# Two-block transformer kernel: norms transposed by a product with a diagonal, scale and shift applied by channel in the split

## The chip, the cores and the metric

The kernel runs as one program on one core of a Trainium2 chip. The metric is the device time of the program in microseconds (us), lower is better. The engines are named as in the profile: PE is TensorE (matmuls), DVE is VectorE, ACT is ScalarE, POOL is GpSimd, SP is SyncE, which here only issues the large weight loads.

## The reference, cut to what matters

Two blocks work on 256 tokens of 1024 channels in float32, one after the other. What is computed, cut to the norms and what stands between them:

```
# block 1, two layers
for l in range(2):
    y = token_mixer(x, ...)                        # attention and mLSTM
    x = layer_norm(ALPHA*x + y, ln_g[l,0], ln_b[l,0])
    y = swiglu(x, w13, w2) if l == 0 else moe_ffn(x, router_w, router_b, exp_w13, exp_w2)
    x = layer_norm(ALPHA*x + y, ln_g[l,1], ln_b[l,1])
# block 2, two layers
for l in range(2):
    x = x + mixer2(rms_norm(x, norm_mix_g[l]))     # conv, attention, gated linear attention
    x = x + conv_ffn(rms_norm(x, norm_ffn_g[l]))
return rms_norm(x, final_g)

layer_norm: (x - mean) * rsqrt(var + eps) * g + b      rms_norm: x * rsqrt(mean(x*x) + eps) * g
```

The mean and variance are taken over the 1024 channels of a token; `g` and `b` are vectors by channel. `moe_ffn` sends each token to 2 of 8 experts by `x @ router_w`.

## The kernel before

**Tiling.** `x` lies in SBUF as two tiles (`t` = 0, 1) of 128 tokens by 1024 channels. A quarter is one `t` and one half `h` of 512 channels (`QUARTERS`). Weights come from HBM in units of 128 partitions by 2048 floats into a ring of six (`raw`, issued by SP, L401), and every unit is split in two f32r parts: `w_hi` by an ACT copy (L1315) and `w_lo` by a DVE subtraction (L1702), in rings of three. `x` is transposed and split likewise into `xT_hi` and `xT_lo`, eight chunks of 128 channels. Every product is three f32r matmuls, hi by hi, lo by hi, hi by lo (L619 to L621).

**Order.** Each engine's instructions stand in the order in which the code writes them; there is no scheduler. Engines meet by semaphores: PE may not start a transpose before `xn_ready`, ACT copies what PE has put in PSUM (`xT_psum`), DVE subtracts what ACT has copied (`xT_hi_ready`), PE takes a chunk when `xT_lo_ready` says so. Splits of the next weight units (`split`) stand between this work at places chosen by hand: `split_next` on ACT splits three units ahead before a norm, and `ahead(14)` splits one before a norm of block 2.

**The norm sites.** Eight places have a norm. After each of them but the last `transpose_x` (L653) has PE make 16 transposes of 128x128 pieces against the identity (`ident`, part of the constants in `cst`) into four PSUM banks, and `x_parts` on ACT (L1330) and DVE (L1712) splits them, four instructions of 128x512 on each. The text calls the sites by letters:

| site | place | norm | about us |
|---|---|---|---|
| A | layer 0 of block 1, after the mixer, ahead of the dense FFN | LayerNorm | 218 |
| B | layer 0 of block 1, after the dense FFN, ahead of the next mixer | LayerNorm | 419 |
| C | layer 1 of block 1, after the mixer, ahead of the router | LayerNorm | 621 |
| D | end of the experts, and entry of block 2 | LayerNorm, then rms norm | 1680 |
| E | layer 0 of block 2, ahead of the conv FFN | rms norm | 1835 |
| F | entry of layer 1 of block 2 | rms norm | 2038 |
| G | layer 1 of block 2, ahead of the conv FFN | rms norm | 2183 |
| H | end of the program | rms norm | 2385 |

**LayerNorm** (`layer_norm`, L1741): after the statistics DVE makes (x - mean) * g on the two quarters of half 0 (`centred`, L1752), takes the reciprocal of the root that ACT made (L1763), makes x * rstd + b on half 0 (`finished`, L1757), and then both for half 1. Each half releases eight transposes. **rms norm** (`rms_norm`, L1770): after each addition of a PSUM quarter to x (L1796) DVE squares and sums that quarter (`mean_square`, L1738); then it adds up the sums (L1773), waits for ACT's root (L1340) and writes `xn` = x * rstd * g, four instructions of 128x512 (L1782), which PE transposes.

**The router** at site C: PE multiplies `xT` by the router's weights, ACT copies the logits (L1504), DVE works out the two experts of every token (L2022 on), and PE gathers the tokens of each expert by a product of `x` with a 0/1 matrix `pick` (L994). This gather is a plain float32 matmul. Ahead of L2022, DVE's queue holds `x_parts` and one weight split.

**Small loads** are issued by POOL in the order of L535 to L606: rows of weights by name into `rows`, `w_if` (runs of four floats), gains and shifts of the norms into `norm_gb` broadcast to all partitions, and the constants of block 2. Most wait for `xn_ready`.

## Time and profile before

| | us |
|---|---|
| the three runs | 2386.18, 2396.31, 2385.08 |
| median | 2386.18 |
| the profiled execution: its own time | 2396.32 |
| its span, first to last instruction | 2394.5 |
| PE busy in it | 2283.5 (95%) |
| DVE busy | 1746.6 (73%) |
| ACT busy | 1322.0 (55%) |
| POOL busy | 181.6 (8%) |
| DMA packets | 423432 for 556.44 MB, 9746 of them under 512 B |

Busy time is the union of an engine's instructions; a busy PE need not be at full speed, since the clock that it was granted is shown beside it (1.00 is 2.4 GHz, 0.50 is 1.2 GHz). A row of the timeline begins with the start in us and the length of the row in us, and ends with the idle time ahead of it and what ended that. A plain float32 matmul leaves two records on PE, so that `x32` at L994 stands for 16 matmuls; a transpose, and each f32r matmul, leaves one.

### The profile page before, as it was taken

What the parts mean: (1) busy time and instruction counts of PE and PEld (TensorE: products, weight loads), DVE (VectorE), ACT (ScalarE), POOL (GpSimd) and SP (SyncE); (2) the same over time, 40 slices, a digit from 0 to 9 for tenths busy, and PEclk for the clock granted to TensorE, in tenths of its full rate; (3) what the DMA queues carried; (4) which work ended last, traced back from release to release, by engine and by line L of the source; (5) the groups of instructions that cost most, each with busy time, mean ns of one, the idle gap of its engine ahead of it and who ended that gap; (6) DMA issues with size and microseconds to landing.
All of it is one profiled execution on the core that took longest, in us unless ns stands there. A gap on an engine that the chain in (4) does not pass through costs nothing.

```text
span 2394.5 us, 41114 instructions
## 1 busy us (share of the span) xinstructions
PE 2283.5 (95%) x16253; PEld 2135.1 (89%) x16253; DVE 1746.6 (73%) x1872; ACT 1322.0 (55%) x1254; POOL 181.6 (8%) x178
## 2 busy tenths in 40 slices
PE   7998999999799999999999999999699999898998
PEld 7998998899799999999999999998687999787997
DVE  4565555557588888888888888887667777767777
ACT  4643433454366767676767776766425444425443
POOL 1000000100000000000000000000580000760000
PEclk9998999999899999999999999999879999989999
DMA  9344655534399999999999999999323555423541
GB/s 304 108 142 141 206 181 175 172 108 143 124 356 335 355 338 349 337 351 336 353 343 348 345 341 349 336 353 329 112 92 117 174 195 174 132 93 126 197 173 56
DMA packets 423432, 556.44 MB, mean 232 GB/s; under 512 B 9746, under 2 KB 377092, under 8 KB 423344
## 3 DMA queue, kind: packets, MB, share of 16 engines
q1 hardware_dynamic: 419232, 544.85, 67.4%
q0 software_dynamic: 4112, 10.38, 1.4%
q8 instruction: 60, 0.98, 0.2%
q14 instruction: 28, 0.23, 0.0%
HBM read 554.13 MB, written 1.06 MB: 232 GB/s over the span
## 4 chain that ended last, share of the span: by engine, by line
issue 45%; PE 42%; DVE 7%; ACT 3%; DVEq 2%; DMA 1%; ACTq 0%; SPq 0%; POOL 0%; POOLq 0%
PE ps L619 12%; PE ps L620 12%; PE ps L621 12%; DVE w_lo L1702 2%; ACT w_hi L1315 2%; PE ps L1191 1%; PE ps L661 1%; DVE cvT L2174 0%; PE ps L1189 0%; DVEq L2175 0%; PE ps L810 0%; DMA raw<-in_w_in 0%; DVE xn L1738 0%; DVE x L1796 0%; PE ps L802 0%
## 5 line engine op out<-in xcount | busy, mean ns | idle before, releaser
L1702 DVE TENSOR_TENSOR w_lo<-raw,w_hi 128x2048 fp32r<-128x2048 f32 x519 | 1180.6, 2285 | 347.1 <-ACT w_hi L1315 345.5
L1315 ACT ACTIVATE w_hi<-raw 128x2048 fp32r<-128x2048 f32 x519 | 987.0, 1908 | 250.7 <-PE ps L621 236.4
L619 PE MATMUL ps<-w_hi,xg_hi 128*128 128x256 f32 x1792 | 516.7, 288 | 2.2 <-DVE w_lo L1702 2.2
L621 PE MATMUL ps<-w_hi,xg_lo 128*128 128x256 f32 x1792 | 505.0, 282 | 0.0
L620 PE MATMUL ps<-w_lo,xg_hi 128*128 128x256 f32 x1792 | 504.8, 282 | 0.0
L619 PE MATMUL ps<-xT_hi,w_hi 128*128 128x256 f32 (+1 forms) x1712 | 493.5, 288 | 11.5 <-DVE xT_lo L1712 6.7
L620 PE MATMUL ps<-xT_lo,w_hi 128*128 128x256 f32 (+1 forms) x1712 | 488.5, 285 | 0.0
L621 PE MATMUL ps<-xT_hi,w_lo 128*128 128x256 f32 (+1 forms) x1712 | 488.2, 285 | 0.0
L619 PEld LDWEIGHTS ps<-xT_hi,w_hi 128*128 128x128 f32 (+1 forms) x1712 | 331.8, 194 | 16.6 <-issue 8.6
L619 PEld LDWEIGHTS ps<-w_hi,xg_hi 128*128 128x128 f32 x1792 | 338.1, 189 | 9.4 <-DVE xg_lo L2086 2.9
L620 PEld LDWEIGHTS ps<-w_lo,xg_hi 128*128 128x128 f32 x1792 | 338.3, 189 | 3.8
L621 PEld LDWEIGHTS ps<-w_hi,xg_lo 128*128 128x128 f32 x1792 | 338.0, 189 | 0.0
L620 PEld LDWEIGHTS ps<-xT_lo,w_hi 128*128 128x128 f32 (+1 forms) x1712 | 331.6, 194 | 1.6
L621 PEld LDWEIGHTS ps<-xT_hi,w_lo 128*128 128x128 f32 (+1 forms) x1712 | 331.2, 193 | 0.3
L619 PE MATMUL ps<-w_hi,hT_hi 128*128 128x512 f32 x536 | 212.8, 397 | 1.0 <-DVE hT_lo L2095 1.0
L620 PE MATMUL ps<-w_lo,hT_hi 128*128 128x512 f32 x536 | 212.0, 396 | 0.0
L621 PE MATMUL ps<-w_hi,hT_lo 128*128 128x512 f32 x536 | 211.6, 395 | 0.0
L619 PE MATMUL ps<-w_hi,xT_hi 128*128 128x256 f32 (+1 forms) x448 | 130.4, 291 | 7.9 <-DVE w_lo L1702 4.3
L620 PE MATMUL ps<-w_lo,xT_hi 128*128 128x256 f32 (+1 forms) x448 | 128.3, 286 | 0.0
L621 PE MATMUL ps<-w_hi,xT_lo 128*128 128x256 f32 (+1 forms) x448 | 128.2, 286 | 0.0
L621 PEld LDWEIGHTS ps<-w_hi,hT_lo 128*128 128x128 f32 x536 | 100.9, 188 | 23.8
L1517 ACT ACTIVATE sa<-ps 128x256 f32<-128x256 f32 x112 | 43.1, 385 | 139.3 <-PE ps L621 139.2
(441 smaller groups left out, 2774.2 us busy)
## 6 DMA issues: line engine op xcount, KB each, us to landing
raw<-in_exp_w SPq DMA_DIRECT2D x336, 1024.0 KB, 6.0
raw<-in_ffn_w_up SPq DMA_DIRECT2D x44, 1024.0 KB, 5.1
raw<-in_w_in SPq DMA_DIRECT2D x42, 1024.0 KB, 6.7
raw<-in_ffn_w SPq DMA_DIRECT2D x33, 1024.0 KB, 5.1
raw<-in_ffn_w_down SPq DMA_DIRECT2D x22, 1024.0 KB, 5.4
raw<-in_w_gate SPq DMA_DIRECT2D x16, 1024.0 KB, 5.3
raw<-in_w_out SPq DMA_DIRECT2D x8, 1024.0 KB, 5.1
raw<-in_w_o SPq DMA_DIRECT2D x6, 1024.0 KB, 6.1
```

The costliest lines, as they stand in the source:

```text
L619: pe.matmul(out, lhs[0], rhs[0], start=first, stop=False)
L620: pe.matmul(out, lhs[0], rhs[1], start=False, stop=False)
L621: return pe.matmul(out, lhs[1], rhs[0], start=False, stop=last)
L661: m = pe.transpose(o[:, c, t, :], src[:, t, (2 * b + c) * P:(2 * b + c + 1) * P], ident)
L1191: m = pe.matmul(o, qgm[rows, h // 2, t, j, :], st8[rows, 4 * t + j, h // 2, :], start=False, stop=j == 3)
L1315: act.activation(w_hi[:, u.const % SPL, 0:width], raw[:, u.const % RAW, 0:width], ACT.Copy)\
L1517: act.activation(sa[:, odd, 0:FFC], ps[:, 6, 0:FFC], ACT.Silu).then_inc(S_.silue_ready, 1)
L1702: dve.tensor_tensor(w_lo[:, u.const % SPL, 0:width], raw[:, u.const % RAW, 0:width], w_hi[:, u.const % SPL, 0:width].bitcast(F32), ALU.sub ...
```

## The change

What it does, by place:

- **PE**: `transpose_x` takes `x` itself, and in place of a transpose against the identity it makes a plain float32 matmul of the piece with `dg[:, t, :]`, a 128x128 diagonal that holds the token's rstd. The very first one of the program (block 1, layer 0) keeps the transpose.
- **DVE, LayerNorm**: (x - mean) * g is made as before. After the first half come two diagonals (`diagonals`), not `finished(0)`. `finished` of all four quarters (`normed_x`) stands behind `x_parts`: right behind it at A and C, behind one more `split` at B.
- **DVE, rms norm**: squares and the four `xn` products go (at H the four products stay); DVE takes one reciprocal and makes one diagonal for each `t`.
- **ACT**: `square_roots` loads the table by a root of a constant, then squares and sums each quarter (Square with an accumulated sum) when DVE has added it, and takes the root.
- **x_parts**: on both engines eight instructions of 128x256, not four of 128x512 (on DVE at the program's start it stays four), with the shift `beta` or the gain `gain` of the channel as bias or scale.
- **D**: the last LayerNorm of block 1 (`last_layer_norm`) releases ACT's squares after each quarter, in the order (0,0), (1,0), (0,1), (1,1).
- **Splits on ACT**: one fewer stands ahead of the norm at B, E, F and G, and that split comes behind `x_parts`.
- **POOL**: four loads of gains to `norm_gb` go, each with its wait; seven loads of vectors by channel (128x8, one float a run) come at the program's start, into `stat`. The loads of the next norm's gain and shift wait for `ln_done`, the load of `final_g` for nothing.
- `zeros`, the width of `stat`, the counts of roots, and some `sem_inc`s whose counts nothing reads are changed as follows from this.

```diff
+            dg = sb("dg", [P, TT, P], scope=shared)
 ...
+                if L == 0:
+                    column = lambda dst, v: pool.dma_start(dst, v.rearrange("(c p) -> p c", p=P), allow_slow_non_contiguous=True)                        .then_inc(S_.beta_loaded, 16)
+                    for n, v in enumerate((A["ln_b"][0, 0], A["ln_b"][0, 1], A["ln_b"][1, 0])):
+                        column(beta(n), v)
+                    for l in range(2):
+                        column(gain(2 * l), A["norm_mix_g_2"][l])
+                        column(gain(2 * l + 1), A["norm_ffn_g_2"][l])
+                pool.wait_ge(S_.ln_done, 2 * L + 1)
 ...
-                pool.wait_ge(S_.xn_ready, L * 4 + 10)
-                pool.sem_inc(S_.pool_passed, 1)
-                pool.dma_start(norm_gb[:, 0, :], over(A["norm_mix_g_2"][L], D)).then_inc(S_.norm2_loaded, 16)
                 pool.wait_ge(S_.xn_ready, L * 4 + 12)
-                pool.dma_start(norm_gb[:, 0, :], over(A["norm_ffn_g_2"][L], D)).then_inc(S_.norm2_loaded, 16)
 ...
-                            m = pe.transpose(o[:, c, t, :], src[:, t, (2 * b + c) * P:(2 * b + c + 1) * P], ident)
+                            piece = x[:, t, (2 * b + c) * P:(2 * b + c + 1) * P]
+                            if plain:
+                                m = pe.transpose(o[:, c, t, :], piece, ident)
+                            else:
+                                m = pe.matmul(o[:, c, t, :], piece, dg[:, t, :], start=True, stop=True)
 ...
+                        if shift is not None:
+                            m = act.activation(o, i, ACT.Identity, bias=shift[:, k:k + 1])
+                        elif scale is not None:
+                            m = act.activation(o, i, ACT.Copy, scale=scale[:, k:k + 1])
 ...
+            def square_roots(count, quarters=QUARTERS):
+
+                act.activation(stat[:, 8:9], ones[:, 0:1], ACT.Sqrt)
+                for q, (t, h) in enumerate(quarters):
+                    at = 122 + 2 * t + h
+                    act.wait_ge(S_.x2_ready, count + q + 1)
+                    act.activation(xn[:, t, h * HALF:(h + 1) * HALF], x[:, t, h * HALF:(h + 1) * HALF], ACT.Square,
+                                   accum_out=stat[:, at:at + 1])
+                    act.drain()
+                    if h == 0:
+                        act.activation(stat[:, 126 + t:127 + t], stat[:, at:at + 1], ACT.Copy, scale=1.0 / D, bias=RMS_EPS)
+                    else:
+                        act.activation(stat[:, 120 + t:121 + t], stat[:, at:at + 1], ACT.Sqrt, scale=1.0 / D,
+                                       bias=stat[:, 126 + t:127 + t]).then_inc(S_.roots_done, 1)
 ...
+                            if shift is not None:
+                                m = dve.scalar_tensor_tensor(xT_lo[:, k, :], i, shift[:, k:k + 1], hi, ALU.add, ALU.subtract)
+                            else:
+                                m = dve.scalar_tensor_tensor(xT_lo[:, k, :], i, scale[:, k:k + 1], hi, ALU.mult, ALU.subtract)
 ...
+            def layer_norm(count, norms, at, n):
+
+                centre(norms, at, n)
+                centred(0)
+                root_ready(count)
+                diagonals().then_inc(S_.xn_ready, 1)
+                centred(1).then_inc(S_.xn_ready, 1)
+
+            def normed_x():
+
                 finished(0)
-                centred(1)
-                dve.drain()
-                finished(1)
+                finished(1).then_inc(S_.ln_done, 1)
 ...
+            def rms_norm(n):
+
+                for t in range(TT):
+                    dve.wait_ge(S_.roots_done, TT * n + t + 1)
+                    dve.reciprocal(col(120 + t), col(120 + t))
+                    dve.drain()
+                    m = dve.tensor_scalar(dg[:, t, :], ident, col(120 + t), None, ALU.mult)
+                m.then_inc(S_.xn_ready, 2)
 ...
                 layer_norm(L * 3 + 2, L * 64 + 32, 72, 4)
-                x_parts(L * 12 + 8, 0)
+                x_parts(L * 12 + 8, 0, beta(2 * L))
+                normed_x()
```

How DVE's queue moves at site C (and, but for the last two rows, at A). Before; `lg` are the router's logits, L1712 is `x_parts`, L1702 a weight split:

```order
L1752 SCALAR_TENSOR_TENSOR x<-x,stat,norm_gb 128x512 x2
L1763 RECIPROCAL stat<-stat 128x2
L1757 SCALAR_TENSOR_TENSOR x<-x,stat,norm_gb 128x512 x2
L1752 SCALAR_TENSOR_TENSOR x<-x,stat,norm_gb 128x512 x2
L1757 SCALAR_TENSOR_TENSOR x<-x,stat,norm_gb 128x512 x2
L1712 TENSOR_TENSOR xT_lo<-ps,xT_hi 128x512 x4
L1702 TENSOR_TENSOR w_lo<-raw,w_hi 128x2048
L2022 TENSOR_TENSOR lg<-ps,rb 128x16
```

And after, on the same engine at the same place; L1789 is `centred`, L1801 the diagonals, L1745 `x_parts`, L1795 `finished`, L1728 the split:

```order
L1789 SCALAR_TENSOR_TENSOR x<-x,stat,norm_gb 128x512 x2
L1784 RECIPROCAL stat<-stat 128x2
L1801 TENSOR_SCALAR dg<-cst,stat 128x128 x2
L1789 SCALAR_TENSOR_TENSOR x<-x,stat,norm_gb 128x512 x2
L1745 SCALAR_TENSOR_TENSOR xT_lo<-ps,stat,xT_hi 128x256 x8
L1795 SCALAR_TENSOR_TENSOR x<-x,stat,norm_gb 128x512 x4
L1728 TENSOR_TENSOR w_lo<-raw,w_hi 128x2048
L2076 TENSOR_TENSOR lg<-ps,rb 128x16
```

The four `finished` have moved from ahead of `x_parts` to between it and the split, and the split and the router's first step stand behind them.

ACT's queue at site E (G is the same), before; L1665 is the last copy of the mixer, L1315 a weight split, L1340 the root, L1330 `x_parts`:

```order
L1665 ACTIVATE yA_hi<-cvT 128x512
L1314 REGISTER_ALU
L1315 ACTIVATE w_hi<-raw 128x2048
L1340 ACT_TABLE_LOAD
L1340 ACTIVATE stat<-stat 128x2
L1330 ACTIVATE xT_hi<-ps 128x512 x4
```

After; L1346 are the squares, L1350 and L1352 the sum of two and the root, L1335 `x_parts`, L1319 the split:

```order
L1691 ACTIVATE yA_hi<-cvT 128x512
L1342 ACT_TABLE_LOAD
L1342 ACTIVATE stat<-cst 128x1
L1346 ACTIVATE xn,stat<-x 128x512
L1350 ACTIVATE stat<-stat 128x1
L1346 ACTIVATE xn,stat<-x 128x512
L1352 ACTIVATE stat<-stat 128x1
L1346 ACTIVATE xn,stat<-x 128x512
L1350 ACTIVATE stat<-stat 128x1
L1346 ACTIVATE xn,stat<-x 128x512
L1352 ACTIVATE stat<-stat 128x1
L1335 ACTIVATE xT_hi<-ps,stat 128x256 x8
```

The split that stood ahead of the norm comes behind the last row, and four squares stand where one root stood.

## Rows read from the trace of the kernel before

**Rows 1.** The page, part 4: the chain of waits that ended last, by engine

```profile
issue 45%; PE 42%; DVE 7%; ACT 3%; DVEq 2%; DMA 1%; ACTq 0%; SPq 0%; POOL 0%; POOLq 0%
```

**Rows 2.** Timeline of DVE and PE at site C: start, length, idle ahead

```profile
622.97 1.42 DVE L1757 SCALAR_TENSOR_TENSOR x<-x,stat,norm_gb 128x512 f32<-128x512 f32 x2
...
624.53 1.94 PE L661 MATMUL ps<-cst,x 128*128 128x128 f32 x8 [5.44 <-DVE x L1757]
...
625.78 1.41 DVE L1757 SCALAR_TENSOR_TENSOR x<-x,stat,norm_gb 128x512 f32<-128x512 f32 x2
...
627.34 1.94 PE L661 MATMUL ps<-cst,x 128*128 128x128 f32 x8 [0.87 <-DVE x L1757]
```

**Rows 3.** Timeline at site C, from the end of x_parts to the gather

```profile
629.95 0.69 DVE L1712 TENSOR_TENSOR xT_lo<-ps,xT_hi 128x512 fp32r<-128x512 f32 x1 [0.16 <-ACT xT_hi L1330]
...
631.75 2.29 DVE L1702 TENSOR_TENSOR w_lo<-raw,w_hi 128x2048 fp32r<-128x2048 f32 x1 [1.11 <-ACT w_hi L1315]
...
633.95 0.17 DVE L2022 TENSOR_TENSOR lg<-ps,rb 128x16 f32<-128x16 f32 x1
```

**Rows 4.** Timeline at site C: the first gather, plain float32 matmuls

```profile
639.09 6.44 PE L994 MATMUL ps<-pick,x 128*128 128x128 f32 x32 [1.76 <-DVE extra_sb L2054]
```

**Rows 5.** Groups by line and form, PE, 700 to 1600 us: the later seven gathers

```profile
L994 PE MATMUL ps<-pick,x 128*128 128x128 f32 x224 | 26.1, 275 | 0.0
```

**Rows 6.** Timeline of DVE and PE at site E

```profile
1834.57 0.68 DVE L1796 TENSOR_TENSOR x<-x,ps 128x512 f32<-128x512 f32 x1
1835.37 0.69 DVE L1738 CUSTOM_DVE_ANT_0 xn<-x 128x512 f32<-128x512 f32 x1
...
1837.12 2.74 DVE L1782 SCALAR_TENSOR_TENSOR xn<-x,stat,norm_gb 128x512 f32<-128x512 f32 x4
1838.68 3.26 PE L661 MATMUL ps<-cst,xn 128*128 128x128 f32 x16 [4.60 <-DVE xn L1782]
```

**Rows 7.** Timeline of DVE and PE at site F

```profile
2037.84 0.68 DVE L1796 TENSOR_TENSOR x<-x,ps 128x512 f32<-128x512 f32 x1
...
2042.37 3.65 PE L661 MATMUL ps<-cst,xn 128*128 128x128 f32 x16 [6.06 <-DVE xn L1782]
```

**Rows 8.** Timeline of DVE and PE at site D

```profile
1690.62 0.16 DVE L1773 TENSOR_REDUCE stat<-stat 128x2 f32<-128x4 f32 x1 [1.88 <-DMA cst<-in_const]
...
1693.51 3.65 PE L661 MATMUL ps<-cst,xn 128*128 128x128 f32 x16 [18.92 <-DVE xn L1782]
```

**Rows 9.** Single lines: length in ns, min, median, max

```profile
L1651 ACT ACTIVATE agT<-cvT x2: 630/630/630, 1808.4 to 2157.0; 128x512 f32<-128x512 f32 x2
...
L2048 DVE TENSOR_SCALAR pick<-cst,slot_of x2: 279/282/285, 637.4 to 637.6; 128x128 f32<-128x128 f32 x2
```

**Rows 10.** Stretches around restarts of PE: busy time by engine, then granted clock

```profile
221.80:228.00 6.20, 5.30 (x24) 4.96 (x25) 5.21 (x8) 2.39 (x4) 2.49 (x4) 0.50 0.27 86
...
1693.50:1699.00 5.50, 5.49 (x26) 5.50 (x27) 4.51 (x8) 3.60 (x5) 3.72 (x8) 0.50 0.32 101
...
1839.30:1842.60 3.30, 3.30 (x18) 3.01 (x15) 2.57 (x6) 2.39 (x4) 0.63 (x1) 0.50 0.21 72
...
2042.30:2047.40 5.10, 5.03 (x24) 5.06 (x25) 4.11 (x8) 3.14 (x5) 3.25 (x7) 0.50 0.33 106
...
2184.00:2187.40 3.40, 0.18 (x2) 0.21 (x3) 2.84 (x8) 0.20 (x1) 0.00 (x0) 1.00 0.00 0
```

**Rows 11.** Stretches at the program's start: last figure GB/s, ahead of it DMA share

```profile
22.00:24.00 2.00, 2.00 (x13) 2.00 (x13) 1.64 (x1) 0.33 (x1) 0.00 (x0) 1.00 1.16 240
24.00:26.00 2.00, 2.00 (x19) 2.00 (x18) 0.65 (x1) 0.00 (x0) 0.00 (x0) 1.00 1.02 107
...
32.00:34.00 2.00, 2.00 (x17) 1.93 (x17) 1.62 (x1) 0.92 (x3) 0.00 (x0) 1.00 1.10 348
```

**Rows 12.** Timeline of DVE and PE at the start: a split, and the float32 matmuls before its products

```profile
32.38 2.29 DVE L1702 TENSOR_TENSOR w_lo<-raw,w_hi 128x2048 fp32r<-128x2048 f32 x1 [7.73 <-ACT w_hi L1315]
...
39.80 1.95 PE L781 MATMUL ps<-wqk,xmT 128*128 128x128 f32 x16
```

More of the change, by code:

```diff
@@ L650, in _, with transpose_x @@
             yM_chunks = [(yM_hi[:, k, :], yM_lo[:, k, :]) for k in range(4)]
-            def transpose_x(src, ready, first):
+            def transpose_x(ready, first, plain=False):
                 for b in range(4):
@@ L1316, in split, with x_parts @@
                    .then_inc(S_.hi_ready, 1)
[L1318 to L1321 removed]
             def used(u):
                 act.wait_ge(S_.unit_used, u.value(plus=SPL + 1))
[L1327 removed]
+            def x_parts(count, first, shift=None, scale=None):
                 for b in range(4):
                     act.wait_ge(S_.xT_psum, count + b + 1)
[L1330 removed]
+                    for c in range(2):
+                        k = 2 * b + c
+                        o, i = xT_hi[:, k, :], bank(first + b, 2, S)[:, c, :]
+                        if shift is not None:
[3 more added lines that the diff above has]
+                        else:
+                            m = act.activation(o, i, ACT.Copy)
+                    m.then_inc(S_.xT_hi_ready, 1)
+            def square_roots(count, quarters=QUARTERS):
[11 more added lines that the diff above has]
+                                       bias=stat[:, 126 + t:127 + t]).then_inc(S_.roots_done, 1)
             def y_parts(first, dst, psum, count, done):
@@ L1384, in out @@
                     act.activation(dst, src, ACT.Copy).then_inc(S_.proj1_out, 1)
-                x_parts(L * 8, 4)
+                x_parts(L * 8, 4, beta(1) if L else None)
+                if L:
+                    split(u + 1)
                 for n in range(2):
@@ L1570, in mixer2 @@
             def mixer2(L, u):
-                square_root(S_.sqrt2_in, S_.sqrt2_out, L * 5 + 1, stat[:, 120:122])
-                x_parts(L * 8 + 16, 4)
+                square_roots(8 * L, QUARTERS if L else NORM_ORDER)
+                x_parts(L * 8 + 16, 4, scale=gain(2 * L))
+                if L:
+                    split(u + 1)
                 def ahead(n):
@@ L1673, in _ @@
             act.activation(bvec[:], ps[0:HA, 0, 0:BUCKET_W], ACT.Copy).then_inc(S_.bvec_ready, 1)
-            for n in range(AHEAD):
-                split(Count(n))
+            split(Count(0))
+            split(Count(1))
             for L in range(2):
@@ new lines, in finished, with diagonals @@
+            def finished(h):
+                for t in range(TT):
+                    m = dve.scalar_tensor_tensor(quarter(t, h), quarter(t, h), col(120 + t), norm_gb[:, 1, h * HALF:(h + 1) * HALF],
+                                                 ALU.mult, ALU.add)
+                return m
+            def diagonals():
+                for t in range(TT):
+                    m = dve.tensor_scalar(dg[:, t, :], ident, col(120 + t), None, ALU.mult)
+                return m
+            def layer_norm(count, norms, at, n):
[4 more added lines that the diff above has]
+                centred(1).then_inc(S_.xn_ready, 1)
@@ L2355, in mixer2 @@
                 dve.drain()
-                x_parts(L * 8 + 28, 0)
+                x_parts(L * 8 + 28, 0, scale=gain(2 * L + 1))
                 ahead(14)
```

170 lines of the change are left out of this document (82 added, 88 removed).

## The prediction

> **What bounds the kernel now.** I read the chain of waits first. It gives 42% to PE and 45% to "issue", time in which an engine waited for nothing that the profile shows, and 7% to DVE [rows 1]; with PE busy 95% of the span, the program is one long row of matmuls with holes. The change touches the holes around the eight norms, so I read next the timeline of DVE and PE there. At C, PE waits 5.44 us for the first finished half of x, and 0.87 us for the second [rows 2]. At E it waits 4.60, at F 6.06, at D 18.92 us [rows 6 to 8]. In every hole what ends last is a DVE product over x. The third view is the granted clock: after each hole PE runs at 0.50 for 3.3 to 6.2 us before it is back at 1.00 [rows 10]. A slow stretch is thus worth about as much as the hole that it follows, and the sum has to price it.
>
> **Two prices for PE.** A transpose leaves one record and a plain float32 matmul two. The later seven gathers are such matmuls at full clock: 26.1 us for 224 records [rows 5], 0.117 each. The first gather at C is mostly at half clock: 6.44 us for 32 [rows 4], 0.20 each. The change makes 16 transposes into 16 plain matmuls at seven sites, 16 more records each: 1.9 us at the full price, 3.2 at the other. I take 1.9, although these records themselves run slow: the clock comes back some microseconds after PE has resumed, whatever it runs, so 16 more records push 16 records of products out of the slow stretch into the full one. Seven sites: 13.1 us lost. If that reasoning fails it is 22.5. In the same way an idle microsecond inside a slow stretch is worth 0.117/0.20, about 0.58, and a slow stretch loses 0.42 of its length.
>
> The Trainium skill, "TensorE: Matmul & The Clock Gate", Terms, says that transpose mode is 4 times faster for float32. Sixteen transposes at half clock took 3.65 us [rows 8], sixteen plain matmuls 6.44 [rows 4], 1.8 times; by the page's factor the extra would be three times mine, 26 us more in all and about 2412. The rows decide, and I leave it one chance in a hundred.
>
> **LayerNorm, A and B.** Ahead of the first transposes, two `finished` (1.42 us [rows 2]) give way to two diagonals, which like L2048 take 282 ns each [rows 9] and overlap: about 0.5. PE resumes 0.9 us earlier. The second half then needs only `centred(1)`, ready while PE is still in the first eight, so the 0.87 us gap goes, worth 0.5. Restarts without a gap were slow for 5.5 and 5.1 us at D and F, the one with a gap at A for 6.2 [rows 10]: 0.9 less, worth 0.4. Gain 1.8, loss 1.9: **−0.1 each**. `finished` itself, 2.9 us, now lies on DVE behind `x_parts`, at A ahead of nothing that is due (DVE waits for ACT's first silu there), at B behind the first split.
>
> **C, the router.** Here `finished` stands ahead of a split and of the router's first step, L2022, which started when that split ended at 634.0 [rows 3]. PE starts 0.9 earlier and has no gap, but 3.2 us of records more, so the last piece of `x_parts`, ended at 630.64, comes about 1.4 later. Then 4 x 0.74 = 2.9 us of `finished`, less the 1.11 us that DVE had idle before the split [rows 3]: 1.4 + 2.9 − 1.1 = 3.2, taken as **−3.0**. From L2022 everything goes through DVE to the gather at 639.09, with no slack on the way. The bounds are 1.8 (`x_parts` not later) and 3.5.
>
> **D.** DVE there waits for the constants of block 2 (1.88 us [rows 8]), which are issued as before, so ACT's squares and the order of quarters gain nothing. From 1690.62 on, a reduction, a sum, a root and two products stood ahead of PE at 1693.51, 2.9 us; now two reciprocals and two diagonals, 1.1. Gain 1.8, loss 1.9: **−0.1**.
>
> **E and G.** The last addition starts at 1834.57 and PE at 1838.68 [rows 6], 4.1 us. Without squares between them the additions follow PE's quarters, and the last starts 0.35 earlier. Behind it come one square (630 ns [rows 9] where DVE took 690), a root, a reciprocal and a diagonal, 0.2 to 0.3 each with the hops between engines: 2.5 us. PE resumes 1.9 earlier, loss 1.9: **0** each; a table load or slower hops could take 0.5 off.
>
> **F.** The additions are held by the squares most: the last one starts at 2037.84, PE at 2042.37 [rows 7], yet PE's last product before them was at 2035.91. They would end about 1.4 earlier, and the chain behind is again 2.5 for 4.5. Resume 3.4 earlier, loss 1.9: **+1.5**.
>
> **H and the start.** At H the reduction and the sum go, **+0.4**. ACT splits x in eight pieces, not four, at the start: **−0.3** at most.
>
> **The clock in shorter holes.** PE now idles about 2.7 us at E, F and G in place of 4.6, 6.1, 4.6. At G the clock was still 1.00 until 2187.40 [rows 10], through the whole hole. If it doesn't fall, the slow stretches of 3.3, 5.1 and 3.3 us go, 4.9 us in all at 0.42. No row has such a restart at such an idle, so the bounds are 0 and 4.9; I take half, **+2.4**.
>
> **Column loads.** Seven loads of 1024 single floats are 7168 runs. Two `w_if` loads of 128x12 runs are the nearest: in 22 to 26 us HBM gave 240 and 107 GB/s where 348 is usual [rows 11], a loss of 2.0 us for 3072 runs, so 4.7 us for 7168 if a run costs the same. The split on DVE at 32.38 ends at 34.67, and its unit is used after 41.5 [rows 12]: 6.8 us of slack hide it: **0**. POOL's later loads gain nothing, since nothing waited for them but at D.
>
> **Moved splits.** ACT's split comes behind `x_parts` at B, E, F and G. Its DVE half stood behind `x_parts` already, so the unit is ready perhaps half a microsecond ahead of PE. Taken as **0**, up to 1.4 late each.
>
> **Sum.** −0.1 −0.1 −3.0 −0.1 +0 +1.5 +0 +0.4 −0.3 +2.4 = +0.7 saved. The profiled execution took 2396.32 us, so it would give 2395.6; it is 10 us above the other two levels of the three runs (2385.08, 2386.18), and against the median of 2386.18 the sum gives **2385.5**.
>
> **Rivals.**
> - The clock doesn't fall at E, F and G: 2.5 more saved, **2383.0**. For it speaks that it fell at G only after PE had resumed; against it that such holes are only guessed at 2.7 us. Chance 0.22.
> - The doubled records cost the slow price, because the clock comes back with the products and not with PE's resumption: 9.4 more, **2394.9**, slower than before. Against it: the gather at C, with nothing but plain matmuls, got its clock back inside its 6.44 us [rows 4] (32 records wholly at the slow pace of 0.21 would be 6.8). It decides if the slow stretches of after are longer than those of before by the 3 us of extra records. Chance 0.12.
> - The column loads starve the weights. It decides from 6.8/4.7, 1.45 times my price for a run; at four times, 18.7 − 6.8 = 12 us, **2397.5**, slower. For it: half the chain is fed by one ring, and single floats are the shortest runs here. Chance 0.08.
> - The moved splits are late at four sites, 1.4 each: **2391**. Chance 0.10.
> - Plain matmuls bring the clock back sooner than transposes. At seven sites the slow stretches would be shorter by the 3.4 us of the transposes, 7 x 3.4 x 0.42 = 10: **2375.5**. Against it: the gather, again plain matmuls alone, was slow for most of 6.44 us [rows 4], no shorter than the 5.5 and 5.1 at D and F, which began with transposes. Chance 0.05. The Trainium skill, "TensorE: Matmul & The Clock Gate", Part 4, states this rule: transposes don't count as busy for the clock. The rows on C against D and F don't bear it out.
>
> **Chances and range.** The forecast has 0.42, and with the rivals and the hundredth above this makes 1.00. 2376 to 2396 takes in the forecast with its bounds (C 1.8 to 3.5, the clock 0 to 4.9), the first, second and fourth rival, and also that a set of runs may sit at the upper of the two levels in part. About 0.5% is what a measurement can tell from no change: below 2374.3 faster, above 2398.1 slower. Faster 0.04 (half of the last rival and tails), slower 0.08 (the column loads at four times and more, the slow price with a late split), the same 0.88.
>
> **What would show it.** PE at L671 with x32 records at seven sites, waits ahead of them of about 4.5 at A to C, 2.7 at E, F and G, no second wait. Granted clock 1.00 through one or two of E, F, G. At C, L2076 on DVE about 3 us later, counted from `centred`, and the gather with it. In 20 to 30 us, lower GB/s, but no wait of PE before 42. Wrong would be: a wait of PE for `w_lo` at the start or behind `x_parts`; slow stretches of over 8 us; holes at E, F, G above 3.5 us because ACT's chain is longer than I count.

## The result

The changed kernel takes 2374.26 us (median of 12 runs, 2370.25 to 2380.74) where the kernel before takes 2388.93 beside it (2384.92 to 2399.71). The medians are 14.7 us apart. The ratio of the runs is 0.9927, with a 95% interval of 0.9911 to 0.9942, so 0.7% faster. The prediction was 2385.5, with a range down to 2376; the result lies below the range, and just beyond 0.5% faster, to which it had given 4 chances in 100.

The profiled execution of after has a span of 2372.6 us, 21.9 less than that of before, and PE is busy 96% of it.

```profile
span 2372.6 us, 41369 instructions
...
PE 2276.7 (96%) x16365; PEld 2133.6 (90%) x16365; DVE 1736.3 (73%) x1853; ACT 1346.5 (57%) x1346; POOL 186.0 (8%) x181
...
PE 88%; DVE 5%; ACT 3%; DVEq 2%; issue 1%; DMA 1%; ACTq 0%; SPq 0%
```

PE has 112 records more, 16 at each of seven sites, as counted, and yet 6.8 us less of busy time. The larger part of that is pace, as the count of slow time below shows. In what follows a hole is idle time of PE, and a slow stretch is one in which the granted clock was 0.50 (1.2 GHz). The first reading of after is where PE restarts, each with the idle time ahead (start, length, group, idle), to set beside [rows 2, 6, 7, 8]:

```profile
623.28 6.14 PE L671 MATMUL ps<-dg,x 128*128 128x128 f32 x32 [4.06 <-DVE dg L1801]
...
1828.17 5.46 PE L671 MATMUL ps<-dg,x 128*128 128x128 f32 x32 [2.46 <-DVE dg L1836]
...
2028.49 3.84 PE L671 MATMUL ps<-dg,x 128*128 128x128 f32 x32 [2.48 <-DVE dg L1836]
...
2165.67 3.84 PE L671 MATMUL ps<-dg,x 128*128 128x128 f32 x32 [2.46 <-DVE dg L1836]
```

C restarts at 623.28 (624.53 before), E at 1828.17 (1838.68), F at 2028.49 (2042.37), G at 2165.67 (2187.22). D, not shown, restarts at 1693.78 (1693.51). So nothing is won up to D, 10.8 us went between D and E and 7.7 between F and G, which hold the two mixers of block 2, and 3.4 between E and F. The shorter holes at E and G are 2.1 of that each. Most of the rest lies in the mixers, where the change touches nothing. At F and G the 32 records take 3.84 us, the full pace; at E 5.46.

What happened in the mixers shows in the granted clock of stretches of the kernel before (bounds, length, busy time by engine, then the clock). These are the state products of gated linear attention, on which PE waits for DVE's states (L2266) and then multiplies small pieces (L1189, L1191), followed by scores and a projection:

```profile
1761.00:1787.50 26.50, 26.14 (x104) 22.12 (x105) 10.31 (x31) 2.98 (x8) 24.15 (x22) 0.50 0.14 43
2112.50:2136.00 23.50, 23.50 (x95) 19.93 (x95) 8.93 (x26) 2.99 (x8) 19.95 (x18) 0.50 0.14 46
```

PE is busy throughout and at half clock, 1.2 GHz, for 26.5 and 23.5 us. In the changed kernel the same work of the first mixer runs at 2.4 GHz but for a stretch just ahead of it:

```profile
1754.70:1761.00 6.30, 6.30 (x33) 6.08 (x32) 5.93 (x9) 0.00 (x0) 6.15 (x4) 0.50 0.46 166
1765.00:1783.00 18.00, 18.00 (x134) 15.85 (x135) 12.30 (x32) 4.94 (x10) 17.27 (x16) 1.00 0.18 60
2099.50:2105.80 6.30, 6.30 (x31) 5.63 (x33) 0.41 (x2) 0.00 (x0) 6.00 (x7) 0.50 0.01 3
2106.50:2114.00 7.50, 7.50 (x49) 6.10 (x48) 6.59 (x7) 2.98 (x8) 7.21 (x7) 1.00 0.00 0
```

The wait of PE ahead of these products and the first of them, before and then after, show it in single rows. Six products of L1191 take 1.65 us in the one and 0.93 in the other:

```profile
1761.36 0.80 PE L1189 MATMUL ps<-vc,atT 128*128 128x128 f32 x2 [3.52 <-DVE st L2266]
1762.08 1.65 PE L1191 MATMUL ps<-st,qgm 64*128 64x128 f32 x6
```

```profile
1764.96 0.49 PE L1193 MATMUL ps<-vc,atT 128*128 128x128 f32 x2 [0.44 <-DVE st L2320]
1765.38 0.93 PE L1195 MATMUL ps<-st,qgm 64*128 64x128 f32 x6
```

I added up, from stretches of 0.5 us, the time in which PE was busy at less than the full clock, by place. A stretch whose end cuts a piece of 0.5 us counts with the whole piece, so that each comes out up to 0.5 us too long. Slow times below are by this count unless another is named.

| PE busy below full clock, us | before | before_again | after | after_again |
|---|---|---|---|---|
| A and B | 13.2 | 13.0 | 8.3 | 9.4 |
| C with the router | 15.5 | 15.0 | 15.1 | 13.3 |
| D | 8.6 | 8.9 | 9.2 | 9.5 |
| E, F, G | 20.6 | 20.1 | 8.0 | 4.0 |
| first mixer of block 2, states | 27.1 | 26.7 | 7.0 | 7.5 |
| second mixer, states | 24.5 | 24.5 | 10.4 | 10.6 |
| elsewhere, all in block 1 | 3.9 | 3.6 | 17.2 | 0 |
| sum | 113.5 | 111.8 | 75.2 | 54.4 |

Of the 38 us between before and after, 34 are the states and 17 the norm sites, and 13 go back: the first profile of the changed kernel has four slow stretches (at 14, 89, 492 and 591 us) where the kernel before has one (at 187), and where its own second profile has none. At the 0.42 that a slow stretch loses, 38 us make 16. PE's idle time fell by 15.1 us (111.0 to 95.9), and 112 records more cost 13.1 at 0.117 each. That makes 18 of the 21.9 us between the two spans; the other 4 are not located.

### The profile page after: what moved, and what is told of

Read it like the earlier page. It is cut to its first block, busy times and chain, and to the rows that moved or that the text cites. A ratio compares the mean times of both kernels' runs of the same rounds, so it can differ in the third digit from the quotient of the medians.

```text
span 2372.6 us, 41369 instructions
## 1 busy us (share of the span) xinstructions
PE 2276.7 (96%) x16365; PEld 2133.6 (90%) x16365; DVE 1736.3 (73%) x1853; ACT 1346.5 (57%) x1346; POOL 186.0 (8%) x181
## 4 chain that ended last, share of the span: by engine, by line
PE 88%; DVE 5%; ACT 3%; DVEq 2%; issue 1%; DMA 1%; ACTq 0%; SPq 0%
PE ps L626 27%; PE ps L628 26%; PE ps L627 26%; DVE w_lo L1728 2%; PE ps L671 2%; PE ps L1000 1%; ACT w_hi L1319 1%; PE ps L1017 1%; PE ps L1195 1%; DVEq L2229 1%; DVE cvT L2228 1%; PE ps L819 0%; DMA raw<-in_w_in 0%; PE ps L1062 0%; PE ps L1063 0%
## 5 line engine op out<-in xcount | busy, mean ns | idle before, releaser
L1728 DVE TENSOR_TENSOR w_lo<-raw,w_hi 128x2048 fp32r<-128x2048 f32 x519 | 1179.6, 2283 | 337.3 <-ACT w_hi L1319 335.7
L1319 ACT ACTIVATE w_hi<-raw 128x2048 fp32r<-128x2048 f32 x519 | 986.5, 1907 | 251.8 <-PE ps L628 233.7
```

Source lines behind the costliest of these rows:

```text
L1319: act.activation(w_hi[:, u.const % SPL, 0:width], raw[:, u.const % RAW, 0:width], ACT.Copy)\
L1728: dve.tensor_tensor(w_lo[:, u.const % SPL, 0:width], raw[:, u.const % RAW, 0:width], w_hi[:, u.const % SPL, 0:width].bitcast(F32), ALU.sub ...
```

## The experiments

Each kernel ran on one chip beside the kernel before; kernels that are compared below were in part measured on different chips, and the lower level of the kernel before, 2383 to 2387, was the same on all of them. Two questions lead: what the states' slow stretches hang on, and what the norms themselves are worth once these are out of the way. Medians are of 6 or 12 runs.

### Is it the same in a second profile

> The kernel before, unchanged, for a second profile. In the first one 27 and 24 us of the state products of gated linear attention (L1189, L1191; 1760 to 1788 and 2112 to 2137 us) ran at granted clock 0.50. Theory 1 (chance): whether the clock falls and stays down there differs from one execution to the next, so this profile may show one or both of these stretches at full clock for most of their length, and the runs lie between 2385 and 2399 us with a mean clock from 0.974 down to 0.968. Theory 2 (fixed by the order of work): both stretches are slow again for over 20 us each and every run has a mean clock near 0.969. Ratio to before 1.000 within 0.003 by both.

Measured: 2391.65 (2383.97 to 2396.53), ratio 1.0002 [0.9983, 1.0021]. The second profile has both long stretches again, within a microsecond of the first two. The runs do not all have them: over all measurements, 98 runs of the kernel before fall into three groups, 5 at 2376 to 2379, 51 at 2383 to 2387, 42 at 2389 to 2400. Steps of 8 to 10 us are what one stretch of 24 to 27 us costs (0.42 of it is 10 to 11). Both profiled executions are of the upper group, so a sum that starts from their rows starts from the slower kind of execution. Theory 2 is wrong as it was put (mean clocks from 0.968 to 0.975), theory 1 isn't shown by the profile alone.

> The changed kernel, unchanged, for a second profile and more runs beside the undone ones. 2370 to 2376 us. Theory 1 (chance): the state products show another pattern of half clock than the 6.8 and 6.8 us of the first profile. Theory 2 (fixed): the same pattern.

Measured: 2374.9 (2368.15 to 2379.24), ratio 0.994 [0.9918, 0.9962]. The same pattern as the first profile near the states: 7.5 and 10.6 us. The 18 runs of the changed kernel spread over 2368 to 2381.

### Undoing one half of the change

LayerNorm undone (`finished` ahead of plain transposes, no shift in the split):

```diff
-                diagonals().then_inc(S_.xn_ready, 1)
-                centred(1).then_inc(S_.xn_ready, 1)
+                finished(0).then_inc(S_.xn_ready, 1)
+                centred(1)
+                dve.drain()
+                finished(1).then_inc(S_.xn_ready, 1)
```

> The changed kernel with LayerNorm at A, B and C as before: finished x ahead of plain transposes, no diagonal, no shift in the split, nothing behind x_parts. If the gain sits in block 2 alone, this keeps it, and the return of about 3 us at C even makes it faster: 2371 to 2374. If the earlier restart and the shorter slow stretches at A and B (10.2 to 6.8 and 10.2 to 3.4 us of half clock in the profiles) are worth more than C costs, it is slower than the changed kernel: 2376 to 2378.

Measured: 2375.88 (2371.01 to 2377.66), ratio 0.9937 [0.9915, 0.9959]. Not told from the changed kernel, but its profile has the long stretch in the first mixer (26.4 us), where the changed kernel has 7.0, so the two differ by more than LayerNorm. Inconclusive; it is repeated below.

rms norms undone (squares on DVE, one root, four products to `xn`, plain transposes):

```diff
-                    m = dve.tensor_scalar(dg[:, t, :], ident, col(120 + t), None, ALU.mult)
-                m.then_inc(S_.xn_ready, 2)
+                for h in range(2):
+                    for t in range(TT):
+                        m = dve.scalar_tensor_tensor(xn[...], quarter(t, h), col(120 + t), norm_gb[...], ALU.mult, ALU.mult)
+                    m.then_inc(S_.xn_ready, 1)
```

> The changed kernel with the rms norms at D, E, F and G as before: squares on DVE, one root, four products to xn, plain transposes of xn; the gain by channel stays in the split, and the products at these sites multiply by an unrelated vector, so these norms are not computed as in the reference. H stays as changed. If the gain comes from the shorter holes at E, F and G (4.6, 6.1 and 4.6 to 2.5 us) and the clock that no longer falls there, this loses about 8 us: 2382 or more, and 3 to 7 us of half clock come back at each of them. If the clock in the state products is set by this change too (they come behind D and F), slow stretches of over 20 us return there and it reaches 2390. If neither, it stays within 2 us of 2374.

Measured: 2391.83 (2388.21 to 2392.79), ratio 1.001 [0.9996, 1.0023]. The whole gain is gone. E, F and G are back at 21 us of slow PE, and the second mixer has its long stretch (24 us at its end, 37 in the part in all), the first has not. Both expectations happened, and this kernel can't separate them.

### Shift block 2 and change nothing else

```diff
+                if L == 0:
+                    dve.drain()
+                    for h in range(2):
+                        dve.tensor_tensor(xn[:, 0, h * HALF:(h + 1) * HALF], quarter(0, h), quarter(0, h), ALU.add)
                 rms_norm(L * 5 + 1, L * 32 + 16, S_.xn_ready, 122, 2)
```

> The kernel before with two additions of 128x512 more on DVE at D (their result is thrown away), ahead of the rms norm, so that everything of block 2 starts about 1.3 us later. Theory alignment: whether PE stays at half clock for 24 to 27 us in the state products depends on where the clock's changes happen to fall against PE's work; a shift alone can then end one of the two long stretches, and the kernel is faster in spite of the added work: 2375 to 2382, mean clock 0.974 or more. Theory structure: the order of work around the wait for the states sets it, and a shift changes nothing: 1.3 us slower than before, both stretches over 20 us.

Measured: 2388.45 (2380.3 to 2390.51), ratio 1.000 [0.9987, 1.0013]. The median didn't fall, so the expected gain isn't there; but 4 of 12 runs are at 2380 to 2381, and the profile is of one of these. It has the same waits of 3.52 and 3.53 us ahead of the states, and only 8.7 and 7.0 us of slow PE there. The same wait can be followed by a long stretch or a short one.

> The kernel before with four such additions, block 2 about 2.9 us later. With two of them 4 of 12 runs were at 2380 to 2381 and 8 at 2387 to 2391, where the kernel before has groups at 2376 to 2379, 2384 to 2387 and 2389 to 2397. Alignment: the shares of the three groups change again, each group about 2.9 us higher. Set by the norms: the same shares as before, 2387 to 2400.

Measured: 2388.02 (2378.93 to 2390.02), ratio 0.9991 [0.9974, 1.0008]. All runs but one lie below 2390 although 2.9 us were added, where 42 of 98 undelayed runs lie at 2389 or above. Had the groups only moved, 42% of the runs would be at 2392 or above, and none is; so the shares changed, as the expectation of alignment has it. Profile: 26.9 in the first mixer, 11.0 in the second.

> The changed kernel with two additions of 128x512 on DVE at D ahead of the reciprocals (result thrown away), so that block 2 starts about 1.5 us later. Alignment: the spread or the level changes by more than the 1.5 us, and some runs have a long slow stretch again: some at 2380 to 2385. Set by the norms: 1.5 us slower than the changed kernel in every run, 2374 to 2377, no long stretch in the profile.

The same edit on the changed kernel, ahead of its reciprocals. Measured: 2381.84 (2378.45 to 2383.72), ratio 0.9975 [0.996, 0.9991]. A delay of 1.4 us costs 7.5. The wait of PE ahead of the state products of the first mixer is 3.51 us again, where the changed kernel had 0.44, and the long stretch is back behind it:

```profile
1763.38 0.80 PE L1193 MATMUL ps<-vc,atT 128*128 128x128 f32 x2 [3.51 <-DVE st L2324]
```

```profile
1762.50:1788.00 25.50, 24.62 (x97) 20.61 (x98) 9.39 (x21) 2.98 (x8) 21.44 (x20) 0.50 0.16 53
```

So what spared the changed kernel the long stretch was the time at which block 2 stood, not anything that its norms do. The traces show one way in which position acts: in both profiles of the changed kernel a slow stretch of 6.8 us lies just ahead (1754.5 to 1761.4 in the first). It made PE late, and a late PE finds the states ready. With the delay no slow stretch lies there, PE comes early, waits 3.51 us and stays slow. A part of the gain is luck of position, and an edit of one microsecond somewhere ahead can take it back.

### Take the wait ahead of the states away

Ahead of the states DVE had, with PE waiting (rows of the kernel before, DVE):

```profile
1747.01 3.19 DVE L1702 TENSOR_TENSOR w_lo<-raw,w_hi 128x2048 fp32r<-128x2048 f32 x1 [0.15 <-issue]
1750.13 4.22 DVE L2174 SCALAR_TENSOR_TENSOR cvT<-avT,cols,cvT 128x256 f32<-128x256 f32 x6
1754.50 2.32 DVE L1702 TENSOR_TENSOR w_lo<-raw,w_hi 128x2048 fp32r<-128x2048 f32 x1
1756.74 0.48 DVE L2264 COPY st<-ps 128x128 f32<-128x128 f32 x2
1757.29 4.01 DVE L2266 SCALAR_TENSOR_TENSOR st<-st,dec,ps 128x128 f32<-128x128 f32 x12
```

Neither the three taps (L2174) nor the second split is needed for the states. The edit moves both behind:

```diff
                 ahead(6)
-                convolve(3)
-                ahead(7)
 ...
                 m.then_inc(S_.state_ready, 1)
+                convolve(3)
+                ahead(7)
```

> The kernel before, with three taps of the convolution and one weight split on DVE moved from ahead of the states (L2264, L2266) to behind them, in both layers of block 2. PE's wait of 3.5 us for the states goes. Theory wait: the idle time ahead of the state products is what lets the clock fall to 0.50 for 24 to 27 us; both long stretches go, 7 us of waits and some 20 us of lost pace: 2360 to 2370. Theory small matmuls: the products with 32 and 64 rows don't hold the clock whatever stands ahead of them; only the waits go: about 7 us faster, 2379 to 2384, with slow stretches of over 20 us in the profile.

Measured on the kernel before: 2370.97 (2367.4 to 2373.13), ratio 0.9934 [0.9919, 0.9949]. Two lines moved give as much as the whole change (15.5 us between the medians), and no run is above 2373.2. PE has no wait for the states in the profile, and 4.8 and 4.0 us of slow time in place of 27.1 and 24.5. The small products hold the full clock once they have it, so theory small matmuls is refuted. Long stretches come behind a wait ahead of them, though not behind every such wait, as before_delay shows.

> The changed kernel with the same move on DVE. Its profiles had 6.8 to 10.2 us of half clock near the states, and waits of 0.44 and 5.3 us. Theory wait: 4 to 9 us faster, 2366 to 2371, no slow stretch there. Theory small matmuls: 3 to 6 us faster, slow stretches stay. If the long stretches are a matter of alignment, one may come back here: 2375 to 2385.

Measured on the changed kernel: 2363.84 (2363.08 to 2367.18), ratio 0.9905 [0.989, 0.9921], 10.4 us below the changed kernel's 2374.26. Its states and what follows run at full clock in both mixers:

```profile
1762.00:1780.00 18.00, 18.00 (x137) 15.85 (x136) 14.64 (x32) 5.38 (x10) 17.41 (x14) 1.00 0.37 118
2080.00:2100.00 20.00, 20.00 (x179) 18.33 (x178) 17.84 (x33) 4.79 (x4) 19.38 (x15) 1.00 0.40 132
```

The spread shrinks too, from 10 us to 4. Position stays a rival here, since the move shifts everything behind it too. All profiles of the case together speak against it. The table has every passage of a mixer of block 2, two in each profile, with the slow time of busy PE in the 32 us behind the first state product, taken from the clock's own changes:

| order on DVE | wait of PE ahead of the states, us | passages | slow PE behind, us |
|---|---|---|---|
| as before | 0.4 to 0.5 | 2 | 0 |
| as before | 1.6 to 2.0 | 5 | 3.4 to 6.8 in four, 23.9 in one |
| as before | 3.5 | 10 | 23.9 to 26.7 in eight, 6.8 and 8.8 in two |
| as before | 4.0 to 5.3 | 3 | 6.7 to 6.9 |
| states first | none, or 1.0 in two | 16 | 0, but for 2.1 in one |

The eight profiles with the states first stand at different positions and none has a long stretch; nine of the 20 passages in the other ten have one. The length of the wait does not order them: two of 3.5 us were followed by short stretches, and the three longest were too. What decides between a long and a short one stays open. The kernels with the states first are the base on which the parts of the change can be priced.

### The parts, priced on that base

> The changed kernel with the states first and the rms norms at D to G as before (squares on DVE, four products to xn by an unrelated vector, so these norms are not computed as in the reference; plain transposes of xn). By the prediction's terms with the clock's bounds the part is worth between 1.4 and 6.3 us: 2365 to 2370. If the rms part carries all of the 7.1 us between before_states_first and states_first: 2371. The 17 us between rms_undone and the changed kernel would then be 7 of this and 10 of one long slow stretch.

Measured: 2367.65 (2366.92 to 2371.96). The rms part is worth 3.8 us, within the 1.4 to 6.3 of the prediction's terms. The 17.6 us between rms_undone and the changed kernel were then 3.8 of this and, at 0.42, 13 of the states (48.5 us of slow PE in the two mixers against 17.4).

> The changed kernel with the states first and LayerNorm at A, B and C as before. Beside states_first (2363.8) it prices the LayerNorm part of the change with the state products out of the way. A and B save slow stretches (10.2 to 6.8 and 10.2 to 3.4 us), C loses about 3: by the prediction's own terms the part costs 3.2 us, so 2360.6 here; with the shorter slow stretches of A and B counted it is about even, 2363 to 2364.

Measured: 2362.19 (2361.0 to 2363.04). The LayerNorm part **costs** 1.6 us; the terms had −3.2. A and B do gain (slow PE of 8.5 us for 13.1), C eats it. The 1.6 us is between two sets of six runs that don't overlap, but it can be off by a slow stretch or two: in the two profiles single stretches of 3.4 us, each worth 1.4, stand at different places (states_first has them at 490, 589, 657 and 1671 us, this kernel at 187 and 1730).

> The changed kernel with the states first and ACT's weight split back ahead of the norm at B, E, F and G. The squares at E, F and G would wait for it: ACT copies a unit for 1.9 us just before the last quarters are added. If ACT's queue is the tight one there, PE resumes up to 1.9 us later at three sites: 2366 to 2370. If there is slack, 2364, or less by the rival of the prediction that the moved splits come late (up to 1.4 at four sites): 2360.

Measured: 2364.3 (2363.07 to 2365.2), as states_first. PE's idle time is 90.5 us here and 90.4 there. ACT has slack for a split on either side. The rival of late splits has no ground, nor does the moved split bring anything.

The rms part gains 3.8 us and the LayerNorm part loses 1.6, so together the two halves are worth 2.2 us here, while before_states_first and states_first differ by 7.1. In the profile of before_states_first PE waits 4.3 us more for the convolution (L1218), which the moved taps now hold up; states_first waits 0.3 there. That covers 4 of the 4.9 us, in one profile of each; the rest isn't located.

### C, the router

The rows of after at C, DVE from the end of `x_parts` on, beside [rows 3]:

```profile
629.44 1.77 DVE L1745 SCALAR_TENSOR_TENSOR xT_lo<-ps,stat,xT_hi 128x256 fp32r<-128x256 f32 x4 [0.59 <-ACT xT_hi L1333]
631.12 2.73 DVE L1795 SCALAR_TENSOR_TENSOR x<-x,stat,norm_gb 128x512 f32<-128x512 f32 x4
633.77 2.28 DVE L1728 TENSOR_TENSOR w_lo<-raw,w_hi 128x2048 fp32r<-128x2048 f32 x1
635.98 0.17 DVE L2076 TENSOR_TENSOR lg<-ps,rb 128x16 f32<-128x16 f32 x1
```

The router's first step is 2.0 us later. Counted from `centred` (L1789 at 621.19, L1752 at 621.41 before), as the prediction would have it, it starts at 14.8 us where it started at 12.5: 2.3 us later (1.9 in after_again), where 3.0 was booked. `x_parts` ended 0.8 later, not 1.4. PE waits 5.36 us at L987, 2.63 before. The split between is not needed until the gather is over, so it can go behind the router's steps:

```diff
             def router():
-                split(Count(MOE_UNIT0 + 2))
 ...
                 dve.memset(gate_of[:, :, 2 * E_N:], 0.0)
+                split(Count(MOE_UNIT0 + 2))
```

> The changed kernel with DVE's weight split at C moved from ahead of the router's first step to behind its last one, ahead of the gather. The step that followed the split (L2076) then starts when x is finished, about 2.3 us earlier, and PE's wait of 5.36 us at L987 becomes about 3.1. If C lost about 3 us as predicted and the rest of the chain is unchanged: 2.3 us faster than the changed kernel, 2372. If something else bounds the chain to the gather, no change.

Measured: 2374.63 (2372.37 to 2376.38), ratio 0.9945 [0.993, 0.9961], no gain in time. The wait at L987 did fall to 3.2 us. But the 2.2 us moved block 2: PE's wait ahead of the states is 3.53 us again, and the profile has the long stretch in the first mixer:

```profile
1759.50:1783.00 23.50, 23.50 (x97) 20.14 (x97) 9.93 (x29) 2.98 (x8) 19.69 (x18) 0.50 0.14 46
```

A gain of 2 us at C was paid back by position. Together with the states it should show:

> The changed kernel with both moves: the states first on DVE in block 2, and the router's steps ahead of the weight split at C. The first took it from 2374.3 to 2363.8, the second took 2.2 us from a wait of PE but was hidden by a slow stretch in the state products. With that stretch out of the way the two add up: 2361 to 2362. If the router's part is hidden by something else: 2364.

Measured: 2359.33 (2358.02 to 2360.94), ratio 0.9881 [0.9861, 0.99]. 4.5 us below states_first, and 26 us below the kernel before beside it. The wait explains 2.2 of the 4.5. In the profiles two slow stretches of 3.4 us that states_first has, at 657 and 1671 us, are missing here, 1.4 us each, which is position again. Slow PE is 55 us in all.

### The column loads, and the last variant

> best1 with two of the three moved taps back ahead of the states: they fit while PE is still in the steps and the next projection. best1 had a new wait of PE for the convolution (L1222, 2.7 us in two), behind which the moved taps stood. That wait goes without a new one for the states: 2357 to 2358. If the states come late by it (wait over 1 us at L1193): 2360 or more.

Measured: 2361.79 (2360.62 to 2362.64), ratio 0.9889 [0.9866, 0.9912]. The wait for the convolution went from 2.7 to 0.4 us, one of 0.96 came at L1193, and the time is 2.5 us worse than best1 (the kernel with both moves), measured on another chip. The profile has 10 us more of slow PE than that of best1, 4.3 us at 0.42, most of it at the start (14 to 24 us), at 89 us and behind F. So this pair doesn't price the taps.

```diff
                 if L == 0:
+                    pool.wait_ge(S_.rows_ready, 1)
                     column = lambda dst, v: ...
```

> best2 with the seven column loads issued on POOL only when the mixer's decay rows are ready, when the weights' ring no longer takes the whole bandwidth. Forecast of the prediction: the loads at the start are hidden, no difference within 1 us. Rival: they hold back the weights, and this is 3 us or more faster than best2.

Measured: 2358.84 (2358.0 to 2363.0), ratio 0.9879 [0.9856, 0.9903], 2.9 us less than best2, between the two expectations. In the profile of the changed kernel the loads show as a dip of bandwidth from 28 to 36 us, and DVE's split is late as expected, still ahead of its use (bandwidth is the last figure; beside [rows 11, 12]):

```profile
28.00:30.00 2.00, 2.00 (x19) 2.00 (x18) 0.00 (x0) 0.00 (x0) 0.00 (x0) 1.00 1.42 221
30.00:32.00 2.00, 2.00 (x19) 2.00 (x18) 0.00 (x0) 0.00 (x0) 0.00 (x0) 1.00 1.52 53
32.00:34.00 2.00, 2.00 (x17) 1.82 (x16) 0.00 (x0) 0.00 (x0) 0.00 (x0) 1.00 1.17 188
```

```profile
37.18 2.29 DVE L1728 TENSOR_TENSOR w_lo<-raw,w_hi 128x2048 fp32r<-128x2048 f32 x1 [12.78 <-ACT w_hi L1319]
...
39.97 1.95 PE L790 MATMUL ps<-wqk,xmT 128*128 128x128 f32 x16
```

The split is 4.8 us later than before, where 4.7 was predicted, and PE does not wait: L790 starts at 39.97, L781 started at 39.80. The start of this split also moves by itself, between 32.35 and 33.35 in kernels without the loads there. In the pair that differs by the loads alone it is 36.82 (best2) and 33.35 (best2_columns_late), 3.5 us. With the loads late the products start at 39.14, against 39.87 in best2: 0.7 us. The two spans are 2.1 us apart, and the other 1.4 is a slow stretch of 3.4 us at 89 us that best2 has and the other kernel has not; before_delay2, which has no such loads, has one at the same place, and nine of the twelve profiles with the loads early have none, so it isn't theirs. The starve rival is dead, and what the loads cost at the start is 0.7 us.

## Why the prediction was wrong

Point by point:

- **What bounds the kernel.** Here is the failed step. "The change touches the holes around the eight norms", and so the clock was read at the norms alone. A slow stretch of 26.5 us stood 70 us behind D, another one behind F, and nearly half of all slow PE time of before lay in them (51.6 of 113.5 us). The sum has no term for them, so it put what the change would do there at nothing. Measured: 34.2 us less of slow PE in the two places, 14 us at 0.42, in the profiles. The argument that a slow stretch is worth about as much as its hole was right and wasn't applied to the wait of 3.5 us ahead of the states, though every edit ahead of it moves it. A prediction would have had to say: two places worth 10 us each hang on position. With that the range would have reached down to 2366.
- **Two prices for PE.** Right. The 32 records took 6.1 us where most of them were at half clock and 3.84 at full, 0.19 and 0.12 each. The rival of the slow price wanted slow stretches longer than before by the extra records, and at A, B and C they are shorter: 4.8, 3.3 and 4.9 us of slow PE from the restart on, where it was 5.5, 7.0 and 5.5 (by the clock's own changes). And with the states settled the rms part gains 3.8 us over its four sites, where the slow price would have left it between a loss of 4 and a gain of 0.9.
- **A and B.** Restart 4.07 and 4.10 us after PE's last product (5.09 and 5.12 before), the gap gone, both as put. The clock came back sooner than I took: slow PE of 13.2 us became 8.3, mostly at B (7.4 to 3.4). At 0.42 that is 2.1 us for both sites, 1.6 in the second profile (9.4), where I had counted 0.4 each: mis-sized by half.
- **C.** The mechanism was right and the size too large: −3.0 was booked, and L2076 came 2.3 us later counted from `centred` (1.9 in the second profile), near the lower bound of 1.8. The gather started 2.7 later by that count and ended only 1.6 later by the clock, since it ran in 5.6 us where it had taken 6.4.
- **D.** The experts' last products began 1.6 us later (L1062 at 1672.97, L1056 at 1671.35), an effect of C, and PE restarted only 0.27 later. From the end of DVE's wait for the constants (1692.76) to PE (1693.78) it was 1.0 us, put at 1.1.
- **E, F, G.** Holes of 2.46, 2.48 and 2.46, put at 2.7. The squares cost ACT 0.63 us and a read of the sum 0.19 us, which I had not counted.
- **The clock in shorter holes.** It stayed at full through F and G, and fell at E. Over the 11 profiles of kernels with this norm it stayed at full behind 18 of 33 such holes of 2.5 us, so that half was a fair guess for the term as it was put. But the three places had 12 to 16 us less of slow PE, 5 to 7 us, where +2.4 was booked and 4.9 was the bound. Part of it is slow time after the norm (4 us each behind E and G before) that I hadn't looked at. The first rival, 2383.0, was nearer than the forecast.
- **Column loads.** The split came 3.5 to 4.8 us later for 4.7 and was hidden but for 0.7 us.
- **Moved splits.** 0. Right.
- **The rival of plain matmuls.** Shorter by 3.4 us at each of seven sites would be 24 us of slow PE, 10 us in time. By the clock's own changes, and counted from the restart on, the seven sites had 35.7 us before and 22.5 after, 5.5 us in time, but six of the holes are shorter too. At D the hole stayed long (17 to 22 us), and all profiles can be compared: PE was slow for 4.3 to 5.8 us behind transposes (seven profiles, mean 5.2) and for 2.9 to 6.1 behind plain matmuls (eleven, mean 4.3), 0.8 less and not 3.4. By the Trainium skill, "TensorE: Matmul & The Clock Gate", Part 4, transposes don't count as busy for the clock. The rows at D don't bear it out. The result of 2374.3 is close to that rival's 2375.5, but by another way: its number was hit by accident.

So the sum over the norms was right to a few microseconds: with the states out of the way the change is worth 2.2 us by its two halves, or 7.1 as a whole, and +0.7 was forecast. What is left of the 14.7 us between the medians, 7.6 to 12.5, comes from a place that the change doesn't touch, and the forecast had it at nothing.

## What to carry to other kernels

Before pricing an edit, list every stretch in which PE is busy at half clock, over the whole program, with the hole ahead of it. Where a long slow stretch of small products follows a hole, an edit far ahead can switch it on or off, and a comparison of two kernels measures that and not the edit. Single slow stretches at other places come and go in the same way, 1.4 us each here, so that a difference of 1 to 3 us between two kernels is not yet a price. Take the hole ahead of a long stretch away first (here by moving work that nobody waits for behind the work on which PE waits), then price the parts; it was also the cheapest gain of the case, 15 us for three moved taps and one moved split in each mixer.

## What the runs showed of the hardware that was not expected

- After a hole of 3.5 us the state products (64 and 128 rows, 128 columns, six in 1.65 us at the slow pace) and what follows them stayed at 1.2 GHz for 24 to 27 us, with PE busy for 26.14 of 26.5 us. Without the hole the same products ran at 2.4 GHz for 18 us and more. In other executions with the same hole the clock was back after 7 to 10 us (before_delay: 3.52 us of wait, 8.7 us slow), and holes of 4.0 to 5.3 us were followed by 7 us. Why it stays down is open.
- The level of a whole kernel moved by 7.5 us for a delay of 1.4 us (after_delay), and a gain of 2.2 us can vanish in a long slow stretch (router_first).
- A hole of 2.5 us left the clock at full at F and G and not at E, in one profile, and at all three in the second profile of the changed kernel; over 11 profiles at 18 of 33. Holes of 4.5 to 6.1 us at the same sites were followed by half clock in 21 of 21.
- 7168 runs of four bytes held a weight split up by 3.5 us (best2 against best2_columns_late) to 4.8 us (after against before), 0.49 to 0.67 ns a run; for 3072 runs of sixteen bytes the bandwidth of [rows 11] gives 2.0 us, 0.65 ns a run.
